# Two output projections of a hybrid encoder step, moved from a three-product split to plain fp32

## The reference: what is computed

```python
# layer 0 (ab_mixer)
out = jnp.concatenate([o_gla, o_gdn], axis=-1) @ w_out      # rows are normalised per head and gated first
# layer 1 (mla_mixer)
return o.reshape(B, L, MLA_H * MLA_V) @ w_out, ckv, kr
# trunk, after each mixer
x = x + gate * out
```

## Time and profile before

| | |
|---|---|
| three runs, median (lowest to highest) | 2626.19 us (2612.37 to 2630.95) |
| the profiled execution, its own time | 2631.12 us |
| its span | 2629.3 us |
| mean granted TensorE clock | 0.87 of full |
| busy share PE, DVE, ACT, POOL | 83%, 63%, 49%, 10% |
| first phase_out, first instruction to the next phase's first | 704.98 to 798.49 us |
| second phase_out | 1843.37 to 1916.44 us |

### The profile page before, as it was taken

One profiled execution on the slowest core, in us unless ns is written; L12 is line 12 of the kernel. 1 busy time (PEld: TensorE's weight loads), 2 busy tenths in 40 slices (PEclk: granted clock), 3 DMA queues, 4 the chain that ended last, 5 costly groups with the idle time before them and its releaser, 6 DMA issues. The chain is left out here.

```text
span 2629.3 us, 32574 instructions
## 1 busy us (share of the span) xinstructions
PE 2175.1 (83%) x12836; PEld 1822.5 (69%) x12836; DVE 1648.5 (63%) x1851; ACT 1295.7 (49%) x1421; POOL 261.2 (10%) x326
## 2 busy tenths in 40 slices
PE   2689769897584799999999087999957999999990
PEld 1689758797484688888887054666846888888870
DVE  0354118644455688888898323544456889888883
ACT  1235511122312677777776242333125777777772
POOL 0122120041000111111100000000001110111100
PEclk6789885698795899999999588988858999999995
DMA  8277440000222699999999504000326999999974
GB/s 322 76 254 257 172 150 1 5 1 5 84 91 95 244 363 371 373 373 385 372 366 321 193 12 155 1 1 1 123 103 243 374 368 366 369 361 371 370 286 162
DMA packets 160168, 561.27 MB, mean 213 GB/s; under 512 B 34012, under 2 KB 40056, under 8 KB 126864
## 3 DMA queue, kind: packets, MB, share of 16 engines
q1 hardware_dynamic: 138064, 538.85, 55.4%
q0 software_dynamic: 21952, 20.32, 2.3%
HBM read 557.65 MB, written 50.70 MB: 231 GB/s over the span
## 5 line engine op out<-in xcount | busy, mean ns | idle before, releaser
L1888 DVE TENSOR_TENSOR ex_wl<-ring,ex_wh 128x2048 fp32r<-128x2048 f32 x384 | 867.9, 2289 | 113.0 <-ACT ex_wh L1843 113.0
L1843 ACT CAST ex_wh<-ring 128x2048 fp32r<-128x2048 f32 x384 | 712.4, 1910 | 0.0
L226 PE MATMUL ex_p<-ex_wh,ex_xh 128*128 128x512 f32 x1024 | 414.7, 405 | 8.3 <-DVE ex_xl L1893 8.3
L226 PE MATMUL ex_p<-ex_wl,ex_xh 128*128 128x512 f32 x1024 | 402.8, 393 | 0.0
L226 PE MATMUL ex_p<-ex_wh,ex_xl 128*128 128x512 f32 x1024 | 402.3, 393 | 0.0
L226 PEld LDWEIGHTS ex_p<-ex_wh,ex_xh 128*128 128x128 f32 x1024 | 194.7, 190 | 46.2 <-DVE ex_xl L1893 9.9
L226 PEld LDWEIGHTS ex_p<-ex_wl,ex_xh 128*128 128x128 f32 x1024 | 194.2, 190 | 42.5
L226 PEld LDWEIGHTS ex_p<-ex_wh,ex_xl 128*128 128x128 f32 x1024 | 194.9, 190 | 36.8
L226 PE MATMUL ex_py<-ex_wh,ex_gh 128*128 128x512 f32 x512 | 200.2, 391 | 2.8 <-DVE ex_gl L1909 2.8
L226 PE MATMUL ex_py<-ex_wl,ex_gh 128*128 128x512 f32 x512 | 200.4, 391 | 0.0
L226 PE MATMUL ex_py<-ex_wh,ex_gl 128*128 128x512 f32 x512 | 200.0, 391 | 0.0
(11 more groups left out here) (397 smaller groups left out, 4045.9 us busy)
## 6 DMA issues: line engine op xcount, KB each, us to landing
ring<-in_moe_w SPq DMA_DIRECT2D x384, 1024.0 KB, 7.2
ring<-in_ada_w SPq DMA_DIRECT2D x24, 2048.0 KB, 12.1
ring<-in_ab_w_in SPq DMA_DIRECT2D x7, 2048.0 KB, 9.8
mod<-mod SPq DMA_DIRECT2D x16, 512.0 KB, 7.5
cb_y<-yrow SPq DMA_DIRECT2D x16, 512.0 KB, 9.8
xres<-x SPq DMA_DIRECT2D x12, 512.0 KB, 3.7
x<-xres SPq DMA_DIRECT2D x12, 512.0 KB, 9.5
ring<-in_ab_w_out SPq DMA_DIRECT2D x2, 2048.0 KB, 11.7
```

The costliest lines, as they stand in the source:

```text
L226: ins = nc.tensor.matmul(out, a, b, start=first and n + m == 0, stop=last and n == len(terms) - 1 and m == 2)
L1843: nc.scalar.copy(part(wh, u), g.view(base + u)).then_inc(hi_ready, 1)
L1888: nc.vector.tensor_tensor(part(wl, u), g.view(base + u), part(wh, u).bitcast(F32), ALU.subtract).then_inc(lo_ready, 1)
```

## The change

Both projections take the transposed rows and the weights as plain fp32. The rows' transposes are copied once to `oT`; the weights are read from the ring where they landed. Units are 512 columns wide, so there are two per projection, one for each ring chunk. The split tiles, the casts and subtractions and their semaphores are gone (three semaphores less per phase), and a ring chunk is now free when the unit that reads it has been multiplied for all five tiles (`y_done`), where it was free after the split. The order of the statements on SP is the same.

```diff
-    UNITS = D // 256
+    UNITS = D // 512
...
-        oh, ol = sb("oh", [P, KT, TOK], F32R), sb("ol", [P, KT, TOK], F32R)
-        y = sb("y", [P, 2, 256])
+        oT = sb("oT", [P, KT, TOK])
+        y = sb("y", [P, 2, 512])
...
-        split = Splits(g, ctx, f"out{s}", [(base + u // 2, 256 * (u % 2), 256 * (u % 2) + 256, (y_done, NT * (u + 1))) for u in range(UNITS)])
+        for u in range(UNITS):
+            g.free_when[base + u] = (y_done, NT * (u + 1))
...
-                def take_lo(t):
-                    tok = slice(t * P, t * P + width(t))
-                    dve.wait_ge(oh_ready, t + 1)
-                    nc.vector.tensor_tensor(ol[:, :, tok], tp[:, t % 2, :, 0:width(t)], oh[:, :, tok].bitcast(F32), ALU.subtract).then_inc(ol_ready, 1)
-
                 def add(u, t):
                     w, c, n = width(t), int(t == NT - 1), u * NT + t
-                    cols = slice(256 * u, 256 * u + 256)
+                    cols = slice(512 * u, 512 * u + 512)
...
-                split.lo(dve, 0)
-                split.lo(dve, 1)
                 dve.wait_ge(par_here, 64 if gated else 32)
...
-                    if t:
-                        take_lo(t - 1)
                     if t >= 2:
                         add(0, t - 2)
-                take_lo(NT - 1)
                 add(0, NT - 2)
                 add(0, NT - 1)
-                split.lo(dve, 2)
                 for u in range(1, UNITS):
                     for t in range(NT):
                         add(u, t)
-                    if u + 2 < UNITS:
-                        split.lo(dve, u + 2)
...
                 if gated:
                     factors(batches[0])
-                split.hi(act, 0)
-                split.hi(act, 1)
-                if gated:
                     factors(batches[1])
...
-                    nc.scalar.copy(oh[:, :, t * P:t * P + w], tp[:, t % 2, :, 0:w]).then_inc(oh_ready, 1)
-                for u in range(2, UNITS):
-                    split.hi(act, u)
+                    nc.scalar.copy(oT[:, :, t * P:t * P + w], tp[:, t % 2, :, 0:w]).then_inc(oT_ready, 1)
...
                     if t >= 2:
-                        pe.wait_ge(ol_ready, t - 1)
+                        pe.wait_ge(oT_ready, t - 1)
...
                 for u in range(UNITS):
-                    wh, wl = split.get(pe, u)
+                    wo = g.chunk(pe, base + u)
...
-                            pe.wait_ge(ol_ready, t + 1)
+                            pe.wait_ge(oT_ready, t + 1)
                         if n >= 4:
                             pe.wait_ge(y_ready, n - 3)
-                        product(nc, py[0:w, n % 4, 0:256], [(oh[:, k, tok], ol[:, k, tok], wh[:, k, :], wl[:, k, :])
-                                                            for k in range(KT)]).then_inc(y_done, 1)
+                        for k in range(KT):
+                            last = nc.tensor.matmul(py[0:w, n % 4, :], oT[:, k, tok], wo[:, k, :], start=k == 0, stop=k == KT - 1)
+                        last.then_inc(y_done, 1)
```

More of the change, by code:

```diff
@@ L1416, in phase_out @@
         py = ctx.enter_context(nc.psum_tensor(f"out{s}_py", [P, 4, 512], F32))
-        (par_here, o_ready, tp_done, oh_ready, ol_ready, y_done, y_ready, x_out, sq_done, ms_ready, rs_ready) = map(sem, (
-            "par_here", "o_ready", "tp_done", "oh_ready", "ol_ready", "y_done", "y_ready", "x_out", "sq_done", "ms_ready",
+        (par_here, o_ready, tp_done, oT_ready, y_done, y_ready, x_out, sq_done, ms_ready, rs_ready) = map(sem, (
+            "par_here", "o_ready", "tp_done", "oT_ready", "y_done", "y_ready", "x_out", "sq_done", "ms_ready",
             "rs_ready"))
@@ L1458, in normalise @@
                     nc.vector.tensor_tensor(ot, ot, gr[0:w, t % 2, :], ALU.mult).then_inc(o_ready, 1)
-                def take_lo(t):
-                    tok = slice(t * P, t * P + width(t))
-                    dve.wait_ge(oh_ready, t + 1)
-                    nc.vector.tensor_tensor(ol[:, :, tok], tp[:, t % 2, :, 0:width(t)], oh[:, :, tok].bitcast(F32), ALU.subtract).then_inc(ol_ready, 1)
                 def add(u, t):
                     w, c, n = width(t), int(t == NT - 1), u * NT + t
-                    cols = slice(256 * u, 256 * u + 256)
+                    cols = slice(512 * u, 512 * u + 512)
                     dve.wait_ge(y_done, n + 1)
                     dve.wait_ge(x_here[t], 16)
-                    ch(nc.vector.tensor_tensor(y[0:w, n % 2, :], py[0:w, n % 4, 0:256], gate[0:w, c, cols], ALU.mult))
+                    ch(nc.vector.tensor_tensor(y[0:w, n % 2, :], py[0:w, n % 4, :], gate[0:w, c, cols], ALU.mult))
                     nc.vector.tensor_tensor(xt[0:w, t, cols], xt[0:w, t, cols], y[0:w, n % 2, :], ALU.add).then_inc(y_ready, 1)
```

## The result

The changed kernel took 2660.27 us, the median of four runs (2655.85 to 2665.26). The kernel before stood at 2624.27 beside it (2612.37 to 2630.95). The ratio is 1.0143, with a 95% interval of 1.0100 to 1.0185: 1.4% slower, where 2660 us was forecast. The profiled execution took 2662.92 us with a span of 2661.0 and a mean granted clock of 0.871.

What follows compares the result with a forecast made beforehand. The prediction took TensorE to bound the body of both projections. Its terms, 7.1 + 8.2 + 2 x 9.5 = +34.3 us on the profiled 2631.1, gave 2660 us on the median's scale, range 2640 to 2674.

Steps and rivals of the forecast that it cites:

- What bounds the kernel: Body of both projections: TensorE's back-to-back products set the pace; PE does not wait for the casts and subtractions.
- Products: Both projections: 160 records 0.429 us apart, 68.6 us per projection at full clock, 12.5 and 12.1 us more than before.
- First projection up to its last product, +7.1: Layer 0: start 0.4 us earlier, gate rows then late; stretch from first to last product 7.5 us longer.
- Second projection, +8.2: Up to its last product: start 3.7 us earlier without the split, stretch of products 11.9 us longer.
- the slow clock: First products of the second projection: over 5 us at a granted clock of 0.50, a loss of 2.6 us.
- this case, at +6.4: Second projection: the clock rises as early as in layer 0, so the term is +6.4 us instead of +8.2.
- The ends, +9.5 each: Last product to next phase: five stores queue behind the last product's wait and two ring loads, +9.5 us per layer.
- Clears and first use of the weights: Phase ends: two semaphore clears move but cancel; later ring loads are covered before the experts first touch weights; no cost.
- The sum: Whole kernel: both projections' terms and both ends add to +34.3 us, giving 2660 us on the median's scale, +1.3%.
- Stores that pass the loads: Rival, phase ends: stores flow beside the loads, each end costs 4.3 us instead of 9.5, time 2650; chance 0.18.
- One record per matmul: Rival, products: each matmul made as one record, 34.3 us per projection, time 2591; chance 0.03.
- A clock at half: Rival, products: the clock stays at half throughout, 68.6 us more in each projection, time 2797; chance 0.02.

Runs made afterwards that it cites:

- plain256: The changed kernel with 256 columns a unit instead of 512, same plain products and loads; one run, 2656.99 us.
- nw_first: The changed kernel with a separate semaphore for the norm weights, so the first row need not wait for the gate rows; 2650.77 us, ratio 1.0084.
- late_loads: The changed kernel with the second chunk's two ring loads left to the next norm's stream; 2636.62 us, ratio 1.0052.
- late_blocked: As late_loads, but SP still waits for the very last product ahead of the five stores; 2648.87 us, ratio 1.0083.
- warm_split512: The kernel before, split kept, with 512 columns a unit, separate norm-weights wait, splits between tiles, and 56 unread transposes starting both norms; 2624.57 us, ratio 0.9997.
- bridge: warm_split512 with 72 unread transposes instead of 56 at the start of both norms, and eight more between the first two tiles'; 2606.26 us, ratio 0.9929.

## Why the prediction was right, step by step

- **What bounds the kernel.** Right for the later units, wrong for the first unit of layer 0. There PE did wait for DVE, three times in the kernel before, and the products behind the last wait ran 3.2 us at a clock of 0.50:

```profile
737.88 1.09 PE L1543 MATMUL out_tp<-cst,ab_o 128*128 128x128 f32 x8 [1.21 <-DVE ab_o L1458]
743.42 0.68 PE L1543 MATMUL out_tp<-cst,ab_o 32*128 32x32 f32 x8 [1.33 <-DVE ab_o L1458]
744.56 0.58 PE L226 MATMUL out_py<-out_wh,out_oh 128*128 128x256 f32 x1 [0.46 <-DVE out_ol L1463]
```

The changed kernel has none of these waits. The sum did not suffer, because the old stretch of 64.6 us was measured with the waits in it; that is mainly why 12.5 us of dearer products became only 7.5 in the stretch.

- **Products.** Right: 160 records per projection, 6.87 us a tile for 16 of them, 0.429 each at a clock of 1.00. plain256 shows that it is the columns that are paid.
- **First projection up to its last product, +7.1.** Measured +7.7: the start moved by 0.2 us (0.4 forecast) and the stretch grew by 7.9 (7.5). That the gate rows are late next is shown by their name at DVE's first row and by nw_first.
- **Second projection, +8.2.** Measured +6.1. The mis-sized term is the slow clock: 2.6 us were taken from this phase's own windows, and 0.6 were lost. The start came 4.1 us earlier (3.7). Two sets of transposes back to back stand ahead of the products now, where there was a pause for the split; the clock was up 2 us into the first tile. The prediction had named this case, at +6.4.
- **The ends, +9.5 each.** The mechanism was right and is shown by late_loads and late_blocked; the size was 10.9 and 11.2 without the clear. The prediction had put both transfers at 423 GB/s. The sag between loads and stores, 1.0 us in layer 0, is most of what was missing.
- **Clears and first use of the weights.** The clears cancel: none stands at the first end, one at the second. Nobody waited for the ring's later loads.
- **The sum.** 34.3 forecast, 35.9 measured in the two phases: 3.1 too little for the ends, 0.6 too little for the first projection, 2.1 too much for the second. In the span 4.2 us came back elsewhere, in phases that the change doesn't touch: the attention phase was 4.3 us shorter, 1.2 of it the clear and the rest at a higher clock, and the other phases gave and took about 1 to 2 us each. No step had them; without them the profiled execution would have stood 4 us higher, still in the range. So it is luck that the median met the forecast to 0.3 us: errors of 3.1, 0.6 and 2.1 us and the 4.2 elsewhere nearly cancel, and the runs themselves lie over 9 us. What was earned is the mechanism and the terms.
- **The rivals.** Stores that pass the loads: against it 14.1 us in place of the 9 at which it would have decided. One record per matmul: 160, not 80. A clock at half: 1.00 in the body.

## What to carry to other kernels

When a split is dropped and its source is read straight from a ring, the ring's slot comes free with the last product and no longer with the split: look at what is queued behind that wait, since here it cost nearly as much as the dearer products (22 us against 25), and one line gave it back. Price a product form by the pace of its own kind elsewhere in the trace. Before a few microseconds are read from medians, look at whether the two kernels ran every stretch at the same granted clock.

## What the runs showed of the hardware that was not expected

The same norm, with PE busy through its transposes and products, ran them at 0.50 in some runs and at 1.00 in others, 34 or 25.5 us. In warm_split512 a pause of 2.5 us behind work at 1.00 was followed by 0.50 for the 23 us of work that remained; in bridge, with pauses of 1.1 and 0.4 us, it stayed at 1.00 up to the last 3 us. The attention phase took 228 to 236 us at mean clocks from 0.90 to 0.87. Loads followed by stores in one queue sagged to 283 GB/s for 3 us, between stretches of 422 and 426. Split records of 512 columns ran 0.232 us apart, of 256 columns 0.118; plain fp32 records took 0.429 and 0.216, in proportion to their columns.
